# Opening of a two-layer kernel: the first w_in row moved to second place in the weight stream, the first K-tile's parts formed between the copies of the turned banks

## The reference, cut to what matters

```python
mod = silu(c) @ w_ada + b_ada                 # (1024,) @ (1024, 6144)
shift1, scale1, gate1, shift2, scale2, gate2 = split(mod, 6)
h = rms_norm(x, norm1_gain) * (1 + scale1) + shift1
proj = h @ w_in                               # (256, 1024) @ (1024, 3592)
```

## Time and profile before

| | before |
|---|---|
| median of three runs | 1671.28 us |
| lowest, highest run | 1668.65, 1673.79 us |
| span of the profiled execution (first to last instruction) | 1673.4 us |
| TensorE busy | 95% of the span |
| mean granted clock of TensorE | 0.979 |

### The profile page before, as it was taken

The page is one execution under the profiler, slowest core; times in us unless marked ns, Lnnn a source line. Parts: engine busy times, 40 slices in busy tenths (PEclk is TensorE's granted clock), DMA queues, the critical chain, the costliest instruction groups (busy, mean ns, idle before and its releaser), DMA issues. The chain is left out here.

```text
span 1673.4 us, 26490 instructions
## 1 busy us (share of the span) xinstructions
PE 1587.1 (95%) x10351; PEld 1426.7 (85%) x10351; DVE 1224.7 (73%) x2475; ACT 906.1 (54%) x1518; POOL 41.7 (2%) x82
## 2 busy tenths in 40 slices
PE   5998888999999999999999999899999898989998
PEld 5877767999999999988888888797888677789997
DVE  5876765889997999867667777657886666654664
ACT  6775455554545555555555555546556646455453
POOL 0023000000000000000000000110000000000000
PEclk9999899999999999999999999999999899999999
DMA  9944343667766555567788767554443122445552
GB/s 327 364 161 128 102 159 125 213 217 235 229 205 213 158 158 151 165 229 248 237 293 289 250 234 245 202 177 151 151 150 128 63 89 101 151 151 177 181 197 101
DMA packets 111665, 313.85 MB, mean 188 GB/s; under 512 B 9441, under 2 KB 10041, under 8 KB 102073
## 3 DMA queue, kind: packets, MB, share of 16 engines
q1 hardware_dynamic: 100008, 276.95, 49.9%
q10 hardware_dynamic: 11040, 33.66, 5.9%
q0 software_dynamic: 496, 1.59, 0.3%
HBM read 293.28 MB, written 18.89 MB: 187 GB/s over the span
## 5 line engine op out<-in xcount | busy, mean ns | idle before, releaser
L300 PE MATMUL ps<-parts,parts 128*128 128x512 f32 (+1 forms) x4992 | 972.4, 357 | 20.1 <-DVE parts L290 18.1
L300 PEld LDWEIGHTS ps<-parts,parts 128*128 128x128 f32 x4992 | 824.3, 191 | 155.9 <-DVE parts L290 19.1
L285 ACT CAST parts<-lead 128x512 fp32r<-128x512 f32 x940 | 579.1, 620 | 619.9 <-PE ps L300 394.1
L290 DVE TENSOR_TENSOR parts<-lead,parts 128x512 fp32r<-128x512 f32 x940 | 641.1, 688 | 328.8 <-ACT parts L285 324.8
L1833 PE MATMUL ps<-parts,parts 128*128 128x256 f32 x3072 | 385.3, 285 | 4.5 <-DVE parts L290 4.5
L1833 PEld LDWEIGHTS ps<-parts,parts 128*128 128x128 f32 x3072 | 372.6, 192 | 5.6 <-DVE parts L290 5.6
L376 PE MATMUL ps<-lead,mem 128*128 128x128 f32 (+2 forms) x292 | 46.5, 323 | 41.0 <-ACT mem L520 23.2
L376 PEld LDWEIGHTS ps<-lead,mem 128*128 128x128 f32 (+2 forms) x292 | 40.9, 162 | 47.5 <-ACT mem L520 24.6
L2010 DVE TENSOR_SCALAR mem<-lead,mem 128x128 f32<-128x128 f32 x256 | 71.1, 341 | 0.0
L1819 PE MATMUL ps<-mem 128*128 128x128 f32 x512 | 67.9, 275 | 0.7 <-DVE mem L2010 0.7
L1819 PEld LDWEIGHTS ps<-mem 128*128 128x128 f32 x512 | 62.8, 192 | 1.2 <-issue 1.1
(11 more groups left out here) (348 smaller groups left out, 994.3 us busy)
## 6 DMA issues: line engine op xcount, KB each, us to landing
lead<-in_peer_expert_down SPq DMA_DIRECT2D x64, 1024.0 KB, 5.5
lead<-in_peer_expert_up SPq DMA_DIRECT2D x64, 1024.0 KB, 5.8
lead<-in_w_in SPq DMA_DIRECT2D x50, 1024.0 KB, 5.2
lead<-in_w_ffn_in SPq DMA_DIRECT2D x22, 1024.0 KB, 5.2
act_spill<-mem ACTq DMA_DIRECT2D x32, 512.0 KB, 5.1
mem<-act_spill ACTq DMA_DIRECT2D x32, 512.0 KB, 3.6
mem<-in_w_ada SPq DMA_DIRECT2D x29, 512.0 KB, 6.9
lead<-in_w_ffn_out SPq DMA_DIRECT2D x11, 1024.0 KB, 4.9
```

The source lines that it names most:

```text
L285: act.copy(w_hi[g % BUFFERS], st.words(n, u * UNIT, UNIT)).then_inc(hi_ready, 1)
L290: dve.tensor_tensor(w_lo[g % BUFFERS], st.words(n, u * UNIT, UNIT), w_hi[g % BUFFERS].bitcast(F32), ALU.subtract).then_inc(lo_ready, 1)
L300: mm = pe.matmul(o, lhs[a], rhs[b], start=start and i == 0, stop=stop and i == 2, skip_group_check=True, **kw)
```

## The change

The ring's order becomes ada0, row0, ada1, row1 | ada2, row2, ada3, row3, ... ada7, row7. On ACT the high part of unit 0 is formed before the first bank is copied, K-tile 0's columns and parts follow the copy of the first bank, and the other three copies come after the high parts of units 1, 2 and 3. On DVE `mods(1)` moves from ahead of `low_part(0)` to behind the low part of unit 1; every later `mods` keeps its place. PE's wait for the four copies moves from before unit 0 to before unit 2, the first that writes banks 4 and 5.

```diff
@@ -255,11 +255,9 @@
-        for k in range(KT + 1):
-            if k < KT:
-                n_ada.append(st.add(1, mod_pair(A["w_ada"], k), D, turned=True)[0])
-            if k:
-                n_wide.append(st.add(1, wide_row(w_in, k - 1, 1536), SLOT))
+        for k in range(KT):
+            n_ada.append(st.add(1, mod_pair(A["w_ada"], k), D, turned=True)[0])
+            n_wide.append(st.add(1, wide_row(w_in, k, 1536), SLOT))
@@ -563,12 +561,11 @@
-            def turn_out(self, act):
-
-                for q in range(4):
-                    act.wait_ge(self.s_t, q + 1)
-                    act.copy(self.turned[:, 2 * q:2 * q + 2, :].rearrange("p k t -> p (k t)"), ps[:, self.bank0 + q, :])\
-                        .then_inc(self.s_out, 1)
+            def turn_out(self, act, q):
+
+                act.wait_ge(self.s_t, q + 1)
+                act.copy(self.turned[:, 2 * q:2 * q + 2, :].rearrange("p k t -> p (k t)"), ps[:, self.bank0 + q, :])\
+                    .then_inc(self.s_out, 1)
@@ -738,10 +735,11 @@
-                pe.wait_ge(norm1.s_out, 4)
                 for k in range(KT):
                     norm1.await_k(pe, k)
                     for c in range(WIDE):
+                        if k == 0 and c == 2:
+                            pe.wait_ge(norm1.s_out, 4)
                         unit(c, n_wide[k][1] + c, k)
@@ -799,11 +797,13 @@
                 for k in range(KT):
-                    if k + 1 < KT:
+                    if 0 < k < KT - 1:
                         mods(k + 1)
                     norm1.low_part(dve, k)
                     for c in range(WIDE):
                         split_lo(dve, n_wide[k][0], n_wide[k][1] + c, c, 0)
+                        if k == 0 and c == 1:
+                            mods(1)
@@ -882,13 +882,16 @@
                 norm1.other_row(act)
-                norm1.turn_out(act)
+                split_hi(act, n_wide[0][0], n_wide[0][1], 0, 0)
+                norm1.turn_out(act, 0)
                 act.wait_ge(s_first, 1)
                 for k in range(KT):
                     norm1.columns(act, k)
                     norm1.parts(act, k)
-                    for c in range(WIDE):
+                    for c in range(0 if k else 1, WIDE):
                         split_hi(act, n_wide[k][0], n_wide[k][1] + c, c, 0)
+                        if k == 0:
+                            norm1.turn_out(act, c)
```

## The result

The changed kernel takes 1681.7 us (median of six runs, 1677.84 to 1685.28) beside 1673.05 us for the kernel before in the same number of runs (1668.65 to 1674.69): the medians are 8.7 us apart. The ratio over all runs is 1.0056 with a 95% interval of 1.0039 to 1.0074, so 0.56% or 9.4 us slower. The forecast was slower, by 12.2 us. The spans of the two profiled executions are 1680.2 and 1673.4.

A forecast was written before the change was run, and what follows sets the result against it. TensorE, busy 95% of the span, bounds the kernel. Despite 2.6 us gained early, late loads start unit 24 10.8 us late; with 1.7 for half clock, +12.2 on the median 1671.3 gives 1683.5 us, range 1673.5 to 1687.

The forecast's parts named there:

- Opening: Start of the kernel: first product from 22.12 to 19.56, unit 4 from 29.60 to 27.0, 2.6 us gained.
- T(0): T(k) is the end of DVE's last split of K-tile k; for K-tile 0 forecast at 23.5 us.
- Order of loads: SP's queue in the loop: ada k+3 goes out with row k+2, wanted 5.1 to 5.7 us later; this decides.
- The size of a turn: DVE and load queue, per two K-tiles: 15.2 us, 10.0 of it landing, where PE needs 11.4.
- rival B: Loop loads: the pair lands in 7.4 us, a turn is 12.6, time 1673.6 to 1675.3; chance 0.15.
- The bias loads: POOL's loads beside ada7, issued at 54.0: they lengthen its landing by 2.0 us (from 1.3 to 3.3).
- The other chain: Loop over odd K-tiles from 28.65: ada4 lands just in time, it stays ahead and doesn't decide.
- The clock: TensorE at half clock after idling: 1.7 us lost, charged once in K-tile 6; before units 8 and 16 hidden.
- signs named beforehand: Right if first product near 19.6, ada3 lands after 9.6 to 10.3, DVE waits 10 to 15 us, unit 24 near 69.
- three late turns: The forecast itself, in the loop: w_ada tiles land late three times, +7.3 to +14.4 us; chance 0.70.
- Rival C: Loop loads: the pair moves at full rate, lands in 6.8 us, +0.9 us, time 1672.2; chance 0.04.
- Rival E: Opening: row0 lands later than 15.35, ACT's first copy starts 0.85 late, time 1684.4; chance 0.05.

The follow-up runs named there:

- e1: The kernel before with only the new order of loads, ACT, DVE and PE as before; ratio to the kernel before 1.0045 (1.0029 to 1.0060).
- e3: The changed kernel, same slots, but SP issues ada k+3 ahead of row k+2 (loads 5 to 14); ratio to the kernel before 0.9985 (0.9972 to 0.9999).
- e4: The changed kernel with mods(1) back ahead of the first low part, loads in the new order; ratio to the kernel before 1.0029 (1.0014 to 1.0044).
- e5: The changed kernel with the release of POOL's bias traffic moved from behind K-tile 3 to behind K-tile 7; ratio to the kernel before 1.0026.
- e6: The changed kernel with PE adding zero products in its idle stretches ahead of K-tiles 2, 5 and 6; ratio to the kernel before 1.0037.
- e7: The kernel before with 14 zero products on PE between its transposes and the first product; ratio to the kernel before 0.9991 (0.9977 to 1.0005).

## Why the prediction was right

The sign, the mechanism and the place of the cause were as forecast; the size was 12.2 us and is 9.4 by the runs, 8.6 by the end of the first stage in the trace. Step by step:

- **Opening.** Forecast: unit 0 at 19.56, T(0) at 23.5, unit 4 at 27.0. Measured: 19.43, about 23.4, 26.75. The copies behind units 1 to 3 and PE's moved wait cost nothing, as said.
- **Order of loads.** Row2 and ada3 leave 0.37 us apart, right behind T(0), and DVE waits. e1 and e3 show it from both sides.
- **The size of a turn.** Here the sum was off. I took 10.0 us from the row's issue to the w_ada landing, with 9.6 and 10.3 as bounds. The two turns from T(0) and T(2) had 8.5 and 7.6, outside these bounds, and the second was that of rival B. So T(2) came at 37.1 instead of 38.7, T(4) at 49.9 instead of 53.9. The bounds came from the staggered pairs of the kernel before, and 10.3 and 9.6 contained the 2.3 us for which the second load hadn't been issued: with an earlier w_ada tile still landing for 2.3 us behind the row's issue (17.27 + 8.8 = 26.1), the staggered pair took 10.3, and the pairs issued together at 37.6 in e1 and at 35.3 in e4, with 2.1 and 2.4 us of an earlier tile left, took 8.0 and 8.6. That speaks for it that issuing it sooner brings it sooner. An earlier tile in the queue seems to have a part too: the one pair of the changed kernel within the bounds, 9.9, was issued at 28.44 with ada3 landing until 31.9. No run separates the two.
- **The bias loads.** Charged at 2.0; measured 2.3 to 3.4 (e5 against e1, e4, e6 and the changed kernel). With it the last turn was about as long as forecast (12.4 us from the row's issue to the landing against 12.0).
- **The other chain.** I wrote that the chain over odd K-tiles doesn't decide. It did in one place: ada6 landed at 52.9, DVE waited 3.00 for it, and unit 20 came 2.15 late. The pair with ada7 was issued while ada6 was landing. At unit 16, where the forecast had a late turn, PE had no idle stretch: DVE waited only 0.28 us for ada5. So the idle stretches stand before units 8, 20 and 24 (2.72, 2.15, 2.06 us) and not before 8, 16 and 24, and the last is 2.06 instead of about 5.
- **The clock.** Charged once, 1.7 us, in K-tile 6. There K-tile 6 took 7.5 us (65.79 to 73.25) against 7.4 forecast. But the half clock of K-tile 2, which I had called hidden, wasn't wholly: e6 gains 2.5 in all, 1.5 of it in K-tile 6 and 1.0 ahead of it.
- **Sum.** Forecast unit 24 at 69.5 and the end of unit 27 at 76.9; measured 65.79 and 73.25. The 3.7 us between are the first two turns, 1.5 and 2.4 shorter than forecast, less the small rest. Of the signs named beforehand two came out otherwise: ada3 landed 8.5 us after row2's issue and not 9.6 to 10.3, and unit 24 started at 65.8 and not near 69.

Part of the hit is luck. The forecast's own range for three late turns, +7.3 to +14.4, reached down to 7.3 only by letting the bias loads and the lower clock cost nothing. Both cost about what was charged or more, and it was the turns, bounded too tightly, that came out short.

Rival C, the full-rate case: the Trainium skill, DMA: Bandwidth & Descriptors, Anatomy of one DMA, gave an estimate of 6.8 us for 2 MB. The section gives its formula for one DMA issued from GpSimd; here SP issues two. The five pairs took 7.6 to 12.4 us, none as little as the estimate, and the one issued at 23.41 took 8.5 although the tile before it had landed at 22.9. The 1.9 us that the rival gave the second tile stands in no row; the two landings of a pair were 2.5 to 2.9 us apart in the first four pairs. Rival E didn't come about: row0 had landed at 13.5 (13.7 was forecast), before ACT wanted it at 14.61.

## What to carry to other kernels

Count a prefetch not by the number of its slots but by the time between the moment the issuing queue may issue a load and the moment it is wanted. A queue that issues in order turns a free slot into a blocked one when an earlier load in its list waits for something later; here the cure was to exchange the order of issue, with the same slots (e3). Before moving work to shorten an idle stretch of TensorE, price the lower clock behind it too: in the first stage it was worth 2.5 us (e7), about as much as the 2.7 us of idle time that the change removed.

## What the runs showed of the hardware that I had not expected

A w_in row followed at once by a w_ada tile landed after 6.0, 5.0 and 5.8 us (issues at 23.4, 37.1 and 44.2), with at most 1.2 us of an earlier load left to land. That is sooner than the 7.8 and 7.1 of the rows whose w_ada tile was issued 2.3 us later; those had been issued with 2.3 and 4.4 us of an earlier load left. That isn't all of it, for the rows issued at 37.6 in e1 and 35.3 in e4, with 2.1 and 2.4 us left, took 5.5 and 6.1; the cause stays open. And an idle stretch of TensorE is not a sure price: stretches of 2.06, 2.15 and 2.72 us were followed by 3.4 us with the lower clock in the changed kernel, one of 2.15 us in e5 was not.
